# One attention schedule exchanged for another, block-diagonal compressed keys, and low parts and a scan end cut into pieces, in a three-layer fp32 transformer kernel

## What is computed

```python
for l in range(2):                       # first block
    h = rms_norm(x, attn_norm_g[l]); proj = h @ w_in[l]
    # q, k, v of three attentions, and iq, ik, iw of an indexer
    moba = softmax(q k^T, causal) v                              # 4 heads
    diff = (softmax(q1 k1) - lam * softmax(q2 k2)) v, then norm   # 4 heads
    dsa  = attention over the top 64 keys by the indexer's score # 4 heads
    x = x + concat(moba, diff, dsa) @ w_out[l]
    h2 = rms_norm(x, ffn_norm_g[l])
    x = x + (silu(h2 @ w_gate[l]) * (h2 @ w_up[l])) @ w_down[l]
# second block: z = rms_norm(x) @ w_in_2, split into three mixers
y_a = gmlp(u, v)
kc, vc = compress(k_cmp), compress(v_cmp)     # 15 blocks of keys and values per group
s_c = q kc^T * scale                          # 16 heads in 4 groups, 15 columns each
y_b = gated sum of softmax(s_c) vc, a selected and a window attention
y_c = scan(a, b_in) * gelu(gate)              # recurrent mixer, 1024 channels
x = x + norm((gates * (y_a @ w_a, y_b @ w_b, y_c @ w_c)).sum() @ w_o)
x = x + norm(ffn(norm(x)))
```

## Time and profile before

| | |
|---|---|
| median of 3 runs | 1277.11 us (1276.97 to 1277.48) |
| profiled execution | 1276.94 us, its span 1275.0 us |
| TensorE busy | 1253.1 us (98%) |
| VectorE busy | 820.5 us (64%) |
| ScalarE busy | 663.3 us (52%) |
| GpSimd busy | 194.5 us (15%) |
| granted TensorE clock, mean | 0.994 |
| HBM | 167 GB/s over the span |

### The profile page before, as it was taken

The page is one execution under the profiler, slowest core; times in us unless marked ns, Lnnn a source line. Parts: engine busy times, 40 slices in busy tenths (PEclk is TensorE's granted clock), DMA queues, the critical chain, the costliest instruction groups (busy, mean ns, idle before and its releaser), DMA issues.

```text
span 1275.0 us, 16911 instructions
## 1 busy us (share of the span) xinstructions
PE 1253.1 (98%) x6430; PEld 1056.7 (83%) x6430; DVE 820.5 (64%) x981; ACT 663.3 (52%) x981; POOL 194.5 (15%) x162
## 2 busy tenths in 40 slices
PE   8999999999999999999999999999999999999998
PEld 6788888888887888888888899888997778888886
DVE  5898655545669866554457754875685687755454
ACT  5667464443556755434435553645556745644443
POOL 5884100000178620000000000000000030000000
PEclk9999999999999999999999997999999999999999
DMA  7523365556353344555564562433234455545551
GB/s 261 189 93 127 133 215 183 195 191 210 137 198 104 108 170 158 210 186 197 176 218 168 196 217 99 149 122 127 102 121 175 168 179 198 193 176 192 197 196 51
DMA packets 34220, 213.12 MB, mean 167 GB/s; under 512 B 4306, under 2 KB 5586, under 8 KB 11507
## 3 DMA queue, kind: packets, MB, share of 16 engines
q1 hardware_dynamic: 34098, 212.21, 47.4%
q0 software_dynamic: 64, 0.13, 0.0%
HBM read 211.28 MB, written 1.05 MB: 167 GB/s over the span
## 4 chain that ended last, share of the span: by engine, by line
PE 89%; DVE 6%; ACT 3%; issue 1%; DMA 0%; SPq 0%; DVEq 0%; ACTq 0%
PE bank L587 25%; PE bank L589 25%; PE bank L588 25%; PE bank L1003 3%; PE bank L694 2%; PE bank L753 2%; DVE wlo L1703 2%; PE bank L713 1%; PE bank L842 1%; ACT probs L1321 1%; PE bank L615 1%; DVE z L2187 1%; PE bank L1113 1%; PE bank L678 1%; ACT whi L1244 1%
## 5 line engine op out<-in xcount | busy, mean ns | idle before, releaser
L1703 DVE TENSOR_TENSOR wlo<-raw,whi 128x2048 fp32r<-128x2048 f32 (+4 forms) x197 | 442.0, 2248 | 242.1 <-ACT whi L1244 240.8
L1244 ACT ACTIVATE whi<-raw 128x2048 fp32r<-128x2048 f32 (+5 forms) x201 | 369.3, 1842 | 133.0 <-PE bank L589 126.1
L587 PE MATMUL bank<-whi,hT_hi 128*128 128x512 f32 (+4 forms) x1040 | 407.4, 392 | 4.1 <-DVE hT_lo L1738 2.2
L589 PE MATMUL bank<-whi,hT_lo 128*128 128x512 f32 (+4 forms) x1040 | 398.3, 383 | 0.0
L588 PE MATMUL bank<-wlo,hT_hi 128*128 128x512 f32 (+4 forms) x1040 | 398.0, 383 | 0.0
L587 PEld LDWEIGHTS bank<-whi,hT_hi 128*128 128x128 f32 x1040 | 196.7, 189 | 43.6 <-issue 5.7
L589 PEld LDWEIGHTS bank<-whi,hT_lo 128*128 128x128 f32 x1040 | 196.5, 189 | 36.4
L588 PEld LDWEIGHTS bank<-wlo,hT_hi 128*128 128x128 f32 x1040 | 197.0, 189 | 32.9
L587 PE MATMUL bank<-whi,mixT_hi 128*128 128x512 f32 (+1 forms) x248 | 95.5, 385 | 3.4 <-issue 3.1
L587 PE MATMUL bank<-whi,ffT_hi 128*128 128x512 f32 x240 | 93.7, 390 | 0.0
L589 PE MATMUL bank<-whi,ffT_lo 128*128 128x512 f32 x240 | 93.5, 390 | 0.0
(11 more groups left out here) (283 smaller groups left out, 1475.6 us busy)
## 6 DMA issues: line engine op xcount, KB each, us to landing
raw<-in_ff_loop SPq DMA_DIRECT2D x90, 1024.0 KB, 4.8
raw<-in_w_groups SPq DMA_DIRECT2D x64, 1024.0 KB, 4.8
raw<-in_w_out SPq DMA_DIRECT2D x8, 1024.0 KB, 5.6
raw<-in_ff_first SPq DMA_DIRECT2D x6, 1024.0 KB, 4.8
raw<-in_w_values SPq DMA_DIRECT2D x8, 728.0 KB, 4.1
raw<-in_w_comp SPq DMA_DIRECT2D x4, 1024.0 KB, 7.0
raw<-in_ff_last SPq DMA_DIRECT2D x3, 1024.0 KB, 6.5
raw<-in_w_values SPq DMA_DIRECT2D x4, 736.0 KB, 6.8
```

Of the source, the lines that this page charges most:

```text
L587: eng.matmul(out, lhsT=hi, rhs=wh, start=start, stop=False)
L589: return eng.matmul(out, lhsT=lo, rhs=wh, start=False, stop=stop)
L1244: eng.activation(whi[j][:, 0:n], raw[j][:, 0:n], ACT.Copy).then_inc(hi_ready, 1)
L1703: eng.tensor_tensor(wlo[j][:, 0:n], raw[j][:, 0:n], whi[j][:, 0:n].bitcast(F32), ALU.subtract).then_inc(lo_ready, 1)
```

## The change

1. TensorE gets five extra transposes of the identity into bank 2 before its first real ones (`WARM_TURNS`).
2. In both first-block layers the lists of TensorE, ScalarE and VectorE are exchanged for others. Dependencies and work stay the same.
3. GpSimd makes the low parts of chunks 18 and 20 in four pieces of 512 columns.
4. At the end of an FFN VectorE splits the turned rows of tile (0, 0) before it adds (1, 0).
5. The compressed keys go into a zeroed tile block-diagonally, even heads' rows in one 16-column half and odd heads' in the other, and the scores are 16 matmuls of 128 rows by 32 columns, half of them between the two row tiles of product (9, 0).
6. The scan end works in halves of four channel tiles; the low part of chunk (25, 1) goes in front of the multiply.

```diff
+WARM_TURNS = 5
...
                     eng.wait_ge(hi_ready, l * CHUNKS1 + i + 1)
-                    eng.tensor_tensor(wlo[j][:, :], raw[j][:, :], whi[j][:, :].bitcast(F32), ALU.subtract)\
-                       .then_inc(pool_lo, 1)
+                    for q in range(4):
+                        cols = slice(q * COLS, (q + 1) * COLS)
+                        ins = eng.tensor_tensor(wlo[j][:, cols], raw[j][:, cols], whi[j][:, cols].bitcast(F32),
+                                                ALU.subtract)
...
-            eng.memset(headsT[:, T2_V:T2_V + 4, :], 0.0).then_inc(blank_ready, 1)
+            eng.memset(headsT[:, T2_KC:T2_V + 4, :], 0.0).then_inc(blank_ready, 1)
...
-            eng.wait_ge(yc_lo, 1)
+            eng.wait_ge(yc_lo, 2)
...
+            for _ in range(WARM_TURNS):
+                eng.transpose(bank[2][:, 0:P], ident[:, :], ident[:, :])
             turn_half(0, 0)
...
-                turn_heads(4, 1); group_scores(1); group_values(0); row_product(6, 0, 1); row_product(6, 1, 0)
-                row_product(6, 1, 1); group_turn(1); group_values(1); group_scores(2); row_product(7, 0, 0)
-                row_product(7, 0, 1); turn_heads(5, 0); row_product(7, 1, 0); row_product(7, 1, 1)
-                turn_heads(5, 1); group_turn(2); mix_turn(0, 0); group_scores(3); mix_turn(0, 1)
-                out_product(0, 0, 0); group_values(2); group_turn(3); out_product(0, 0, 1); group_values(3)
+                group_turn(0); row_product(6, 0, 0); turn_heads(3, 1); row_product(6, 0, 1); turn_heads(4, 0)
+                turn_heads(4, 1); group_scores(1); group_values(0); row_product(6, 1, 0); row_product(6, 1, 1)
+                row_product(7, 0, 0); group_turn(1); row_product(7, 0, 1); group_values(1); group_scores(2)
+                row_product(7, 1, 0); turn_heads(5, 0); turn_heads(5, 1); row_product(7, 1, 1); group_turn(2)
+                mix_turn(0, 0); mix_turn(0, 1); group_scores(3); out_product(0, 0, 0); group_values(2)
+                group_turn(3); out_product(0, 0, 1); group_values(3); out_product(1, 0, 0); mix_turn(1, 0)
...
+            def compressed_scores(r):
+
+                eng.wait_ge(read67[0], 7)
+                for i in range(8):
+                    g = i // 2
+                    mm = eng.matmul(bank[2 + r][:, i * 32:(i + 1) * 32], lhsT=headsT[:, i, r * P:(r + 1) * P],
+                                    rhs=headsT[:, T2_KC, g * 32:(g + 1) * 32], start=True, stop=True)
                 mm.then_inc(cs_ready, 1)
+
+            product_chunk(9, 0, between=lambda: compressed_scores(0))
+            compressed_scores(1)
             product_chunk(9, 1)
...
+                attend_exp(A + 1, 1); copy_z(l, 6, 0); scale_heads(l, 3); copy_z(l, 6, 1); split_hi(t0, 17)
+                blend_copy(A + 1); split_hi(t0, 18); diff_stats(l, 1); attend_exp(A + 2, 0); copy_z(l, 7, 0)
+                heads_copy(l, 5, 0); split_hi(t0, 19); copy_z(l, 7, 1); heads_copy(l, 5, 1); blend_copy(A + 2)
+                turned_hi_copy(l * 3 + 1, mixT, halves=(0,)); attend_exp(A + 3, 1, in_bank=False)
...
-                turned_hi_copy(l * 3 + 1, mixT, halves=(1,)); split_hi(t0, FFN1); split_hi(t0, FFN1 + 1)
-                turned_hi_copy(l * 3 + 2, hT, halves=(0,))
+                turned_hi_copy(l * 3 + 1, mixT, halves=(1,)); split_hi(t0, FFN1)
+                turned_hi_copy(l * 3 + 2, hT, halves=(0,)); split_hi(t0, FFN1 + 1)
...
-            eng.activation(headsT[:, T2_KC, 0:COMP // 2], bank[6][:, 0:COMP // 2], ACT.Copy).then_inc(read67[0], 1)
+            eng.wait_ge(blank_ready, 1)
+            for odd in range(2):
+                half = slice(HD * odd, HD * odd + HD)
+                ins = eng.activation(headsT[half, T2_KC, 0:4 * 32].rearrange("p (g o n) -> p g o n", o=2, n=16)[:, :, odd, 0:CMP],
+                                     bank[6][half, 0:COMP // 2].rearrange("p (g n) -> p g n", n=CMP), ACT.Copy)
...
-            eng.wait_ge(yc_ready, 1)
+            hi2(26, 0)
             eng.wait_ge(used, done_at(T2, chunk2(23, 1)))
-            eng.activation(mixT[0][:, :, :], headsT[:, 0:8, :], ACT.Copy).then_inc(yc_hi, 1)
-            hi2(26, 0); branch_gate(25, 0); branch_gate(25, 1); hi2(26, 1)
+            for h in range(2):
+                eng.wait_ge(yc_ready, h + 1)
+                eng.activation(mixT[0][:, 4 * h:4 * h + 4, :], headsT[:, 4 * h:4 * h + 4, :], ACT.Copy).then_inc(yc_hi, 1)
+            branch_gate(25, 0); branch_gate(25, 1); hi2(26, 1)
...
                     for n, r in ((0, 0), (0, 1), (1, 0), (1, 1)):
+                        if n and not r:
+                            turned_lo_copy(following, hT, halves=(0,), rows=(0,))
                         whole(2 * n + r)
...
                         gain_rows(r, n)
-                        if n and not r:
-                            turned_lo_copy(following, hT, halves=(0,), rows=(0,))
...
-            for odd in range(2):
-                eng.wait_ge(cs_ready, odd + 1)
-                for r in range(RT):
+            for r in range(RT):
+                eng.wait_ge(cs_ready, r + 1)
...
+            lo2(25, 1)
             dve.wait(eng)
-            eng.tensor_tensor(headsT[:, 0:8, :], headsT[:, 0:8, :], headsT[:, 8:16, :], ALU.mult).then_inc(yc_ready, 1)
-            lo2(25, 1)
...
+            for h in range(2):
+                c = 4 * h
+                eng.tensor_tensor(headsT[:, c:c + 4, :], headsT[:, c:c + 4, :], headsT[:, c + 8:c + 12, :], ALU.mult)\
+                   .then_inc(yc_ready, 1)
...
+            scanned_lo(0)
+            lo2(26, 0)
+            scanned_lo(1)
+            lo2(26, 1)
```

More of the change, by code:

```diff
@@ L968, in _ @@
-                row_product(4, 0, 1); group_scores(0); row_product(4, 1, 0); row_product(4, 1, 1)
-                row_product(5, 0, 0); row_product(5, 0, 1); turn_heads(3, 0); row_product(5, 1, 0)
-                group_turn(0); row_product(5, 1, 1); turn_heads(3, 1); row_product(6, 0, 0); turn_heads(4, 0)
-                turn_heads(4, 1); group_scores(1); group_values(0); row_product(6, 0, 1); row_product(6, 1, 0)
-                row_product(6, 1, 1); group_turn(1); group_values(1); group_scores(2); row_product(7, 0, 0)
@@ L978, in _ @@
-                turn_part(l * 3 + 2, 0, 1); out_product(1, 1, 1)
+                row_product(2, 0, 0); row_product(2, 0, 1); row_product(2, 1, 0); row_product(2, 1, 1)
+                turn_heads(0, 0); row_product(3, 0, 0); turn_heads(1, 0); turn_heads(0, 1); row_product(3, 0, 1)
+                index_scores(l, 0); index_scores(l, 1); index_scores(l, 2); row_product(3, 1, 0)
+                index_scores(l, 3); row_product(3, 1, 1); index_scores(l, 4); turn_heads(2, 0)
+                index_scores(l, 5); row_product(4, 0, 0); turn_heads(2, 1); row_product(4, 0, 1)
@@ new lines, in _ @@
+                group_scores(0); row_product(4, 1, 0); row_product(4, 1, 1); row_product(5, 0, 0)
+                row_product(5, 0, 1); row_product(5, 1, 0); row_product(5, 1, 1); turn_heads(3, 0)
+                group_turn(0); row_product(6, 0, 0); turn_heads(3, 1); row_product(6, 0, 1); turn_heads(4, 0)
+                turn_heads(4, 1); group_scores(1); group_values(0); row_product(6, 1, 0); row_product(6, 1, 1)
+                row_product(7, 0, 0); group_turn(1); row_product(7, 0, 1); group_values(1); group_scores(2)
@@ L1104, in _ @@
             mm.then_inc(filled, 1)
-            product_chunk(9, 0)
-            eng.wait_ge(read67[0], 7)
-            for odd in range(2):
-                half = slice(HD * odd, HD * odd + HD)
-                for r in range(RT):
-                    for i in range(8):
-                        g = i // 2
-                        mm = eng.matmul(bank[2 + odd][:, r * P + i * 16:r * P + i * 16 + CMP],
-                                        lhsT=headsT[half, i, r * P:(r + 1) * P],
-                                        rhs=headsT[half, T2_KC, g * CMP:(g + 1) * CMP], start=True, stop=True)
+            def compressed_scores(r):
[4 more added lines that the diff above has]
+                                    rhs=headsT[:, T2_KC, g * 32:(g + 1) * 32], start=True, stop=True)
                 mm.then_inc(cs_ready, 1)
+            product_chunk(9, 0, between=lambda: compressed_scores(0))
+            compressed_scores(1)
             product_chunk(9, 1)
```

84 lines of the change are left out of this document (41 added, 43 removed).

## The result

The changed kernel takes 1279.88 us, median of 10 runs (1277.57 to 1281.97); the kernel before, on the same chip, 1277.35 (1276.22 to 1277.68, 10 runs). The ratio is 1.0021, 95% interval 1.0011 to 1.003: slower, by about the 0.2% that a measurement here can tell. Forecast were 1266.8 us, and 1262.5 to 1271.0. The forecast is 13 us too low, and its sign is wrong.

The account below looks back on a forecast made before the run. TensorE, busy 98%, was taken as the bound. Gains of 7.4 (scores), 1.7 (layer starts), 0.8 (attention), 0.5 (scan end) and -0.1 (warm turns) sum to 10.3 us: 1266.8 us from 1277.11, range 1262.5 to 1271.0.

Parts of the forecast that it names:

- (d): Attention, wait at 124.6 us: GpSimd's pieces shorten the top-k mask from 3.93 us; up to 0.9 charged beside the blend.
- rival C: Compressed scores: the clock falls again around the softmax waits, 1.7 us lost, 1268.5 us; chance 0.12.
- Scores: Compressed scores: 32 wider records in 3.6 us, clock staying up, chunk (10,0) starting earlier; 7.4 us gained.
- rival E: Compressed scores: wider records cost 0.216 us each, 3.3 us less gained, 1270 us; chance 0.03.
- Attention: New attention order: of 4.65 us of gaps per layer only 0.4 comes back, 0.8 us in both layers.
- (a): Attention, gap of 0.95 us at 93.3 us, between turn_heads(4,*) and group_scores(1): stays.
- (b): Attention, gap at 105.8 us between group_turn(1) and group_values(1): a row product covers the copy, 0.88 us gained.
- (c): Attention, group_turn(2): too little work ahead of it to cover softmax and blend; stalls 0.8 plus 0.7, 1.5 us lost.
- Rival D: Attention: the new order stalls more than counted, 2 us lost a layer instead of 0.4 gained, 1271.6 us; chance 0.06.
- Rival F: Attention: slower than before, as GpSimd's pieces alternate with VectorE's blend and mask, over 5.2 us a layer; chance 0.02.
- Rival B: Opening: warm turns work, bringing full clock before the first matmuls; 1.8 us more gained, 1265 us; chance 0.33.
- Costed at nothing: Larger GpSimd memset, chunk 22's later high part, and early attention swaps of turns and products: no cost, 0 us.

Follow-up runs that it names:

- e3: Changed kernel with only ScalarE's high part of chunk 19 moved later, behind the copies of product 7, heads 5, blend and mixT: 1267.07 us.
- e11: Changed kernel with only chunk 19's load put ahead of SyncE's wait for GpSimd's last gain product: 1271.48 us.
- e7: Kernel before with only the block-diagonal compressed keys and their scores: 1270.46 us.
- e14: e11 with 8 unused matmuls added before group_turn(2) in each layer: 1266.58 us.
- e4: Changed kernel without the five warm turns: 1278.7 us.
- e1: Changed kernel with all three attention lists of the kernel before, all other edits kept: 1262.93 us.
- e5: e1 with GpSimd's low part made in one instruction again instead of four pieces: 1267.66 us.
- e8: Changed kernel with unused matmuls added in each layer, 8 before group_turn(2) and 7 before mix_turn(0,1): 1271.26 us.
- e6: e1 without the five warm turns: 1261.61 us.

## Why the prediction was wrong

**The step that failed** is (d) of the attention order: "group_scores(3) runs 122.3 to 124.6, since ScalarE copies product 7 and heads 5 first; [...] so no stall". ScalarE does not copy heads 5 first: in the new list the high part of chunk 19 stands between the two parts of heads 5, ahead of the copy of product 7's second row tile, and I took its data as given. Up to there the walk was right: `group_turn(2)` was to end near 120.9, and the next turns start at 121.05, with the 0.2 of the opening in it. The data hang on SyncE's queue, whose loads of chunks 19 and 20 stand behind a wait for GpSimd. The profile of before showed the issue at 114.04 and I did not read it, because nothing waited for it there. e3 and e11 undo this from the two ends, ScalarE's place and SyncE's, and both take the wait away. In the changed kernel it is 1.64 us in layer 0 and 2.91 in layer 1, and it comes with the next point, a term that I put at nothing without a reason.

**The clock.** I asked at the scores and at the softmax waits whether the clock would fall (rival C), and not in attention, where I had forecast 1.5 us of waits between small matmuls. Rival C's "1.7 us of wait at 124.6 did not lower it" was one execution's luck: in e7 the same wait in layer 1, with wide products behind it, is followed by 3.4 us at 1.2 GHz. In the new order the places are worse: behind `group_turn(2)` come four transposes, the second wait, four more transposes and the head scores, and only then wide products. Layer 0 adds up: waits 4.65 us before (0.95, 0.88, 0.45, 1.73, 0.64) and 5.02 after (0.95, 1.94, 0.49, 1.64), so 0.4; 13.65 us at 1.2 GHz, about 2.1 of them waits, cost half of 11.5, 5.8; the opening 0.2; 6.4 in all, measured 5.7. Layer 1: waits 6.3, so 1.6, and half of 10.7, 5.4: 7.0, measured 6.9. So the clock is most of the loss. These are estimates, from half the time that the low stretches hold beside their waits; the experiments bear them out: without the wait for chunk 19 the kernel takes 1271.48 us (e11), with the first wait filled too 1266.58 (e14). So 8.4 us hang on the wait for chunk 19 and 4.9 on the clock behind the first wait. Why a fall lasts 3, 7, 10 or 13.65 us was not found.

**Term by term.**
- Scores, 7.4: right, 7.6 in a profiled execution; 5.6 between medians. A record takes 0.112 us, so 3.6 for the 32, as I took it, and neither 3.4 nor rival E's 0.216. During the scores the clock is 1.00 in every profiled execution with them. Behind them it fell once, in e4, for 3.4 us from 788.8, which costs 1.7: rival C as it stands, in one profiled execution out of fourteen.
- Layer starts, 1.7: right, 0.94 each by the same measure, so 1.9.
- Attention, 0.8 gained: 12.6 lost, the opening's 0.2 in it. (a) stayed at 0.95. (b) was right, no wait there. (c) was right: 1.5 and the 0.9 that (d) charges for the pieces beside the blend make 2.4, measured 2.43, and the two stretched instructions are the 0.84 of it that the pieces cost. In (d) the pieces did what was said; the walk behind them was wrong. Rival D had the sign and 0.06 of the chance, and even it stopped at 2 us a layer. Rival F had "slower", with 0.02, but put it down to the pieces, which cost 0.84 us a layer here and gain 4.7 in all with the old lists.
- Scan end, 0.5: VectorE won the race for (26,1), whose low part began at 1042.19 and took 2.29 us, so the upper bound of 1.5; 1.7 between the two marks.
- Warm turns, -0.1: -1.2 and -1.3 by two pairs of medians from different batches; in the traces 0.2 at the opening and 1.1 by the unexplained wait in the second block. Rival B, 0.33: full clock before the first product in three profiled executions of nine, but not in the changed kernel's.
- Costed at nothing: for the memset and chunk 22 no cost was seen, as said. The sentence left out chunks 17 to 19, whose high parts had moved too.

With the attention lists left as they were, the forecast's other terms sum to 9.5; e1 gained 14.0, and the pieces, 4.7 by e5, fill the difference. I had counted them only inside the new order.

## What to carry to other kernels

When a list is reordered, walk every instruction that moves forward back to its data: a high part moved up by 3 us is a transfer needed 3 us earlier, and the queue that issues it may stand in a wait for a quite different engine, harmless until then. Price a forecast wait twice on TensorE, once as time standing still and once as what the matmuls behind it cost at the lower clock: look whether a second wait follows. One trace in which the clock held does not show that it will: compare the mean clock over several executions. Judge the parts of a bundle one by one: here five gained 14 us and one list order took 17.

## What the runs showed that was not expected

- Adding 15 unused matmuls a layer made the kernel 8.6 us faster (e8; 7 by the ratios); in its profiled execution TensorE stays at 2.4 GHz over the whole of attention.
- Stretches at 1.2 GHz of 13.65 us (changed kernel) and about 10 us (e4) start at waits of 1.9 and 0.49 us that lie 0.4 us of transposes apart or soon behind them, when another of 1.6 us or more follows 2 us later; with the same first waits and none behind (e11), four executions had a mean clock of 0.994 and two of 0.998 and 0.999, 5.5 us apart.
- The clock also fell, for 3.4 us, behind waits that it had stood in the other traces: 1.5 us of idle time before the first out product (e7, layer 1) and 1.1 us before chunk (10,0) (e4).
- The kernel before itself varies by 4 us (1274.17 to 1278.25), together with its mean clock; e6, whose clock stays up, varies by 0.1.
